# A two-layer diffusion trunk on one core: expert value rows fetched in blocks of 32 slots of four tokens, and the row slots dealt anew to the stages

## The reference, cut to what matters

```
h = layer_norm(x) * (1 + scale_a) + shift_a
t = token_mix(h)                  # attention | retention | RWKV-7 scan, gates, branches, output
x = layer_norm(ALPHA*x + gate_a*t)
h = layer_norm(x) * (1 + scale_f) + shift_f
x = layer_norm(ALPHA*x + gate_f*peer(h))
```

```
ts, ti = top_k(scores, 16)                       # of 128 keys, two halves per head
fs, fpos = top_k(ts[0] + ts[1], 16)              # of the candidate sums
eidx = picked index; g = softmax(fs)             # (n, 128)
act = gelu(einsum('nkd,nd->nk', u[eidx], x)) * g # a product per slot
out = einsum('nk,nkd->nd', act, v[eidx])         # weighted sum of v rows
```

## Time and profile before

| | |
|---|---|
| median of 3 runs | 4228.18 us (4217.14 to 4244.32) |
| the profiled execution, time of its run | 4215.97 us |
| its span | 4214.2 us |
| moved by its transfers | 1077.41 MB, 256 GB/s over the span |
| TensorE, VectorE, GpSimd busy | 63%, 50%, 42% |
| u fetches, v fetches | 768 each |

### The profile page before, as it was taken

How to read it: one execution, slowest core, us unless ns; L and a number is a source line. 1 busy time by engine, 2 the same in 40 slices (tenths; PEclk the granted TensorE clock), 3 DMA queues, 4 the chain that set the end, 5 groups by cost and what they waited for, 6 DMA issues and landing times.

```text
span 4214.2 us, 52812 instructions
## 1 busy us (share of the span) xinstructions
PE 2670.3 (63%) x21467; PEld 1660.6 (39%) x21467; DVE 2117.1 (50%) x5314; ACT 550.1 (13%) x1415; POOL 1749.7 (42%) x1738
## 2 busy tenths in 40 slices
PE   5878478488977344556788737847897400455576
PEld 1767456366743234112354225636674200000011
DVE  4352588743033899455511168874403699433201
ACT  0231111321000010021010011132100100000000
POOL 1000355322322356666644445542232356666564
PEclk9989689599988666677899868968998755677799
DMA  8506678544866779987989867853486578999897
GB/s 320 200 5 237 165 282 313 191 141 152 295 217 225 264 267 344 347 306 274 322 314 360 293 175 282 308 203 127 152 296 224 182 227 289 347 331 322 299 349 279
DMA packets 346467, 1077.41 MB, mean 256 GB/s; under 512 B 30466, under 2 KB 34696, under 8 KB 346096
## 3 DMA queue, kind: packets, MB, share of 16 engines
q0 software_dynamic: 231168, 829.37, 56.5%
q1 hardware_dynamic: 115056, 244.66, 16.1%
HBM read 1070.24 MB, written 3.67 MB: 255 GB/s over the span
## 4 chain that ended last, share of the span: by engine, by line
PE 37%; DVE 23%; DMA 22%; POOL 10%; issue 5%; ACT 2%; SPq 0%; DVEq 0%; ACTq 0%
DMA arena<-in_peer_v,arena 14%; PE ps L2123 10%; POOL arena L1998 9%; DVE arena L2050 7%; PE ps L1551 5%; PE ps L568 5%; DMA arena<-in_peer_u,arena 3%; DMA ring<-in_w_mod 3%; PE ps L1564 2%; DVE arena L1844 2%; PE ps L1577 2%; PE ps L1279 1%; PE ps L1660 1%; DVE arena L1838 1%; PE ps L1287 1%
## 5 line engine op out<-in xcount | busy, mean ns | idle before, releaser
L1998 POOL DMA_INDIRECT arena<-in_peer_u,arena x768 | 875.9, 1141 | 753.6 <-DVE arena L2050 464.8
L1998 POOL DMA_INDIRECT arena<-in_peer_v,arena x768 | 752.6, 980 | 1041.8 <-PE ps L2123 811.9
L2050 DVE CUSTOM_DVE_ANT_1 arena<-arena,hT 128x1024 f32<-128x1024 f32 x768 | 922.4, 1222 | 437.5 <-DMA arena<-in_peer_u,arena 427.6
L2123 PE MATMUL ps<-arena 128*32 128x512 f32 x3072 | 825.3, 692 | 495.3 <-DMA arena<-in_peer_v,arena 406.1
L568 PE MATMUL ps<-hT,ring 128*128 128x256 f32 (+1 forms) x2496 | 499.8, 366 | 268.7 <-DVE arena L592 259.0
L2123 PEld LDWEIGHTS ps<-arena 128*32 128x32 f32 x3072 | 140.8, 117 | 1091.6 <-issue 508.0
L568 PEld LDWEIGHTS ps<-hT,ring 128*128 128x128 f32 x2496 | 434.3, 221 | 328.2 <-DVE arena L592 265.3
L1551 PE MATMUL ps<-hT,ring 128*128 128x128 f32 (+1 forms) x1536 | 261.2, 329 | 2.6 <-DMA ring<-in_w_in 1.3
L1551 PEld LDWEIGHTS ps<-hT,ring 128*128 128x128 f32 x1536 | 231.8, 191 | 47.8 <-issue 26.9
L1598 DVE TENSOR_TENSOR arena<-ps,arena 128x128 f32<-128x128 f32 (+1 forms) x32 | 11.5, 358 | 389.5 <-PE ps L1564 389.5
L2024 DVE TENSOR_TENSOR arena<-ps,gate 128x512 f32<-128x512 f32 x12 | 8.3, 692 | 389.8 <-PE ps L2123 389.6
(11 more groups left out here) (342 smaller groups left out, 3602.1 us busy)
## 6 DMA issues: line engine op xcount, KB each, us to landing
ring<-in_w_in SPq DMA_DIRECT2D x60, 2048.0 KB, 11.2
ring<-in_w_mod SPq DMA_DIRECT2D x24, 2048.0 KB, 9.2
ring<-in_w_br SPq DMA_DIRECT2D x12, 2048.0 KB, 12.0
ring<-in_w_out SPq DMA_DIRECT2D x8, 2048.0 KB, 12.4
ring<-in_peer_wq SPq DMA_DIRECT2D x8, 2048.0 KB, 9.6
arena<-in_peer_u,arena POOLq DMA_INDIRECT x768, 6.4
arena<-in_peer_v,arena POOLq DMA_INDIRECT x768, 6.2
ring<-in_w_in SPq DMA_DIRECT2D x4, 1536.0 KB, 15.2
```

Of the source, the lines that this page charges most:

```text
L1998: pool.indirect_dma_start(rowbuf[i % NB], None, v_rows if which else u_rows, bass.IndirectOffsetOnAxis(ap=offset, axis=0))\
L2050: nc.vector.tensor_tensor_reduce(row, row, tile_cols(hT, t), 1.0, 0.0, ALU.mult, ALU.add, row_dot[t][:, k:k + 1]).then_inc(sem("u_used"), 1)
L2123: ins = nc.tensor.matmul(row_acc[c][32 * g:32 * g + 32, :], strip[j % 2][:, g, 31 - j:63 - j], rows[g][:, 512 * c:512 * (c + 1)], start=(j ...
```

## The change

A v fetch now takes, instead of 128 slots of one token, 32 slots of each of four tokens: partition 32b+i gets slot 32q+i of token 32b+j, which is what VectorE's 32 x 32 block transpose of the picks gives. So block q of a tile needs only the picks and weights of slots 32q to 32q+31. Quad n of a tile is in block n//8, and the first stands in slot 43 instead of 143. The transposes on TensorE go; VectorE transposes blocks of picks (24 of them, L1948 of the new file) and of weights (24, L2078), and writes the strip (192 times, 16 numbers per partition, L2087) that ScalarE wrote. Since the rows of the accumulators now stand in another order, ScalarE copies them out (2 copies per tile) and 8 more products per tile with rows of the unit matrix put them in order. END is 175 for p's experts and 315 for s's. The table of stages:

| stage | in s mixes, slots before | now | in p1, before | now |
|---|---|---|---|---|
| mod | none | none | none | 0 to 24 |
| projection | 0 to 110 | 0 to 42 | 0 to 150 | 24 to 122 |
| retention | 110 to 130 | 42 to 46 | 150 to 180 | 122 to 132 |
| preparation | 130 to 142 | 46 to 48 | 180 to 200 | 132 to 138 |
| scan | 142 to 192 | 48 to 100 | 200 to 260 | 138 to 198 |
| merge | 192 to 280 | 100 to 180 | 260 to 420 | 198 to 318 |

```diff
+    parts["block"] = p[:, None] // 32 == np.arange(4)[None]
...
-RIDE = {"s": {"proj": (0, 110, 39), "ret": (110, 130, 2), "prep": (130, 142, 3), "scan": (142, 192, 24), "merge": (192, 280, 60)},
-        "p": {"proj": (0, 150, 39), "ret": (150, 180, 2), "prep": (180, 200, 3), "scan": (200, 260, 12),
-              "merge": (260, 420, 60)}}
+RIDE = {"s": {"mod": (0, 0, 10), "proj": (0, 42, 39), "ret": (42, 46, 2), "prep": (46, 48, 3), "scan": (48, 100, 24),
+              "merge": (100, 180, 60)},
+        "p": {"mod": (0, 24, 10), "proj": (24, 122, 39), "ret": (122, 132, 2), "prep": (132, 138, 3), "scan": (138, 198, 12),
+              "merge": (198, 318, 60)}}
...
@@ pe_mod and dve_mod, likewise on GpSimd and ScalarE @@
             for c in chunks:
+                pump("dve", "mod", c)
                 dve.wait_ge(sem("mod_mm"), 12 * l + c + 1)
...
-                nc.vector.tensor_scalar(row_f[t][:, TOPK * h0:TOPK * (h0 + nh)], ij[:, 0, :], float(l * NKEYS * NKEYS),
-                                        None, ALU.add)
                 nc.vector.tensor_scalar(row_no[t][:, TOPK * h0:TOPK * (h0 + nh)], ij[:, 0, :], float(l * NKEYS * NKEYS),
                                         None, ALU.add).then_inc(sem("chosen"), 1)
+                dve.wait_ge(sem("chosen"), at("chosen", u + 1))
+                for q in range(h0 // 2, (h0 + nh) // 2):
+                    cols = slice(32 * q, 32 * q + 32)
+                    nc.vector.transpose(row_noT[t][:, cols], row_no[t][:, cols]).then_inc(sem("no_T"), 1)
...
-            def turn_at(t):
-
-                return 134 + 140 * t
-
-            def quad_at(t, j):
-
-                return turn_at(t) + 6 + 4 * j + 3
+            def start_at(t, q):
+
+                return P * t + 32 * q + 40 + 12 * t
+
+            def quad_at(t, n):
+
+                q, i = divmod(n, 8)
+                return start_at(t, q) + 4 * i + 3
...
-                return 32 * (m % 4) + m // 4
-
-            END = quad_at(nt - 1, 31) + 3
+                q, n = divmod(m, 32)
+                return 32 * q + 8 * (n % 4) + n // 4
+
+            END = quad_at(nt - 1, 31) + 8
...
@@ dve_rows @@
-                        if v == turn_at(t) + 2:
-                            dve.wait_ge(sem("rows_T"), at("rows_T", t + 1))
-                            nc.vector.tensor_copy(row_noT[t], row_acc[0][:, 0:P]).then_inc(sem("no_T"), 1)
-                        if v == quad_at(t, 31) + 1:
+                        for q in range(4):
+                            if v == start_at(t, q) - 3:
+
+                                cols = slice(32 * q, 32 * q + 32)
+                                dve.wait_ge(sem("row_w"), at("row_w", 8 * t + 2 * q + 2))
+                                link(nc.vector.transpose(row_wT[t][:, cols], row_dot[t][:, cols]))
+                        for n in range(32):
+                            if v == quad_at(t, n) - 3:
+                                if 32 * t + n >= 2:
+                                    dve.wait_ge(sem("v_used"), at("v_used", 32 * t + n - 1))
...
+                                nc.vector.tensor_tensor(strip[n % 2][:, :, 28:32], w.to_broadcast([P, 4, 4]),
+                                                        K("block").rearrange("p (o g) -> p o g", o=1).to_broadcast([P, 4, 4]),
+                                                        ALU.mult).then_inc(sem("strip"), 1)
+                        if v == quad_at(t, 31) + 5:
                             residual(t)
...
@@ act_rows @@
+                        if v == quad_at(t, 31) + 1:
+                            act.wait_ge(sem("v_used"), at("v_used", 32 * (t + 1)))
...
+                            for c in range(2):
+                                nc.scalar.activation(sums[c], row_acc[c][:, :], ACT.Copy).then_inc(sem("sum_out"), 1)
...
@@ pe_rows @@
-                                                               strip[j % 2][:, g, 31 - j:63 - j],
+                                                               strip[n % 2][:, g, 28 - 4 * i:60 - 4 * i],
...
+                        if v == quad_at(t, 31) + 3:
+                            pe.wait_ge(sem("sum_out"), at("sum_out", 2 * t + 2))
+                            for c in range(2):
+                                for g in range(4):
+                                    ins = nc.tensor.matmul(row_acc[c][32 * g:32 * g + 32, :], unmix[:, g, :], sums[c],
+                                                           start=True, stop=True, tile_position=(0, 32 * g))
+                            ins.then_inc(sem("sum_in"), 1)
```

More of the change, by code:

```diff
@@ L347, in pool_params, with act_mod @@
                         .then_inc(sem("param_in"), 16)
+            for c in MOD_PARTS[l, part]:
+                pump("pool", "mod", c)
+        def act_mod(act, l, part, pump):
+            for c in MOD_PARTS[l, part]:
+                pump("act", "mod", c)
         def pe_cond(pe):
@@ L2192, in _ @@
             act_cond(act)
[L2193 removed]
+            program("act", act, act_mod, linker(act, "act"))
         @block.vector
```

65 lines of the change are left out of this document (28 added, 37 removed).

## The result

The median went from 4224.97 us (15 runs, 4214.52 to 4244.32) to 4264.41 us (15 runs, 4248.0 to 4277.13): a ratio of 1.009, with a 95% interval of 1.0077 to 1.0104. The change makes the kernel 0.9% slower, 39 us, where 99 us less were forecast. The 4264 us lie outside the range of 4020 to 4215.

A forecast was written before the change was run, and what follows sets the result against it. No one resource was taken to bound the whole: VectorE, TensorE or transfers by stage, transfers in p1 and the last experts. Terms -24 (s0, s1), -37 (p1), -38 (last experts) gave -99: 4117, as a median 4129 us, range 4020 to 4215.

The forecast's parts named there:

- Part 1, projection, retention, preparation: Mixes s0 and s1, each: projection 45 us shorter, retention 20 shorter, preparation 3 longer.
- Part 1, scan: Scan of s0 and s1: u products mostly hidden, fetches with six buffers charged, +25 us each, bounds 0 and 68 + 58.
- (d): Rival: scan of s0 and s1 stops on its fetches, +126 us there and +30 in the gates; 4341 us, chance 0.09.
- the cycle of a quad with six buffers: Scan of s0 and s1: 12.7 us with eight buffers plus two issues of 0.94, so 14.6 us, times 13 = 190.
- Part 1, merge: Gates and rest of s0 and s1: more fetches beside the gate weights, fewer quads behind the scan, +25 us each, bounds 0 and 45.
- Part 2: Mix p1: slots moved into the mod stage, later stages at assumed transfer rates, 1115 us to 1078, -37 us.
- (b): Rival: p1's stages keep their old transfer rates, so p1 gains nothing, +13 us; total 4179 us, chance 0.15.
- Part 3: Last experts: 725 us instead of 767 from slot 43 to the last quad, +4 at the end; -38 us.
- The tail: End of the last experts: two copies and eight products between the last quad and the residual, +4 us.
- Behind it transfers bound, 328 GB/s: Last experts, behind the first quad: transfers taken as the bound, 328 GB/s while u and v fetches alternate.
- Small things: Whole program: strips and block transposes on VectorE, about 41 us, hidden where it waits; bounds 0 and 41 us longer.
- (e): Rival: selection on VectorE delays issuing of fetches, 51 us each in the last experts and p1; 4231 us, chance 0.06.

The follow-up runs named there:

- the short products: Changed kernel with the u products of p's experts cut to 16 of 1024 columns, fetches and waits kept: 4206.1 us in one run, scan of s0 228 us.

## Why the prediction was wrong, step by step

The traces differ by +58 us where the working had -99, so 157 us are to be explained: 85 of them are the scans of s0 and s1, 35 p1 and 37 the last experts.

**Part 1, projection, retention, preparation.** Right: -48 against -45, and -13 against -17. The wait that was to shrink did (TensorE, 457 to 696 us, beside the earlier trace rows):

```profile
PE ps L579 <- DVE arena L603: 27.5, 2, 27.1
```

**Part 1, scan.** This is the step that failed first and most: "+25" was +70 in s0 and +65 in s1. The rival of the slower side, (d), named the mechanism, and it came at a part of its price: scan and gates together cost 105 and 98 us, where (d) had 156. It was given a chance of 0.09. The term that was too small is the cycle of a quad with six buffers, 14.6 us; 17.0 were measured. The working took the cycle of eight buffers and added two issues at 0.94, but from one issue to the next GpSimd takes 1.24. The loop itself, added up anew, is five such steps, landing and the last products, 5 x 1.24 + 5.7 + 1.9 = 13.8 us. The same sum gives 15.8 for five buffers (a landing and a u product come in: 5.7 + 1.2 + 1.24 + 5.7 + 1.9; measured 19.7), 11.8 for half rows in six (14.0) and 9.3 in eight (12.5): 2 to 4 us low each time, with steps between them that go the right way. The rest is not taken apart by any run; the waits of GpSimd for u products, of up to 15.7 us, suggest that VectorE and TensorE come to a landed row only between steps of the levels. 13 x 17.0 is 221 of the 233 us of the window: the scan goes at the pace of the fetches. Had VectorE's work been the cause, the short products would have given back more than 13.

**Part 1, merge.** Right in sum: gates +35, the rest -12, against +25.

**Part 2.** The mod stage +49 against +40, projection -1 against +6, retention and preparation -111 against -108: right. Scan and merge fell short: 192 and 362 us where 173 and 347 were forecast, so -2 instead of -37. The working let them run at 328 and 334 GB/s; they had 293 and 317. For the merge rival (b), that p1 keeps its rates, is what came (361 us); the scan was longer than even (b)'s 177. With buffers freed by row p1 takes 1046 us with the same bytes and order of fetches, so it was not the transfers that could give no more.

**Part 3.** Here nearly all of the forecast failed to come: -38, and the last experts gave 1. From slot 43 to the last quad's end it took 758.6 us, where 725 were forecast and 767 had been. Of the 34 us 11 are the alternating quads (49 at 13.02 and 12.78 instead of 12.7), 8 the turn from one tile to the other (32 us instead of 24), 7 the 13 quads alone, which came every 6.6 us instead of 6.04, and 7 the first quad, which the sum left out: it has 62 of the 64 quads. The tail took 31 us instead of 23, where +4 was forecast. The start of GpSimd's first store, of the changed kernel:

```profile
4259.02 0.58 POOL L2208 DMA_DIRECT2D out<-X  x1 [24.89 <-DVE X L2099]
```

and of the kernel before:

```profile
4205.69 0.58 POOL L2181 DMA_DIRECT2D out<-X  x1 [21.49 <-DVE X L2070]
```

The step from the last quad to it grew from 14.3 to 17.4 us, about as forecast. From the first store to the end it is 13.7 us instead of 8.5, but the stores landed after the same 5.1 and 3.0 us in both kernels. What grew is the closing drain of GpSimd's queue behind them, 7.6 us instead of 2.4. It is 7.6 us in every run with the new fetches and 2.4 in both without; what makes it so is open.

Behind the size stands a reading. "Behind it transfers bound, 328 GB/s" took a rate for a limit because the transfers were busy at 0.92. With buffers freed by row the same transfers moved 386. What the fetches had was eight buffers, each used once a cycle; the cycle was set by the loop above, and the rate came out of it: 8 x 0.524 MB in 12.7 us is 330 GB/s. A run of u fetches at 1.79 us (179/100) had little to gain from such a cycle at 1.6 a fetch, and that was in the rows. The rates of p1 in Part 2 rest on the same reading.

The Trainium skill's limit of about 358 GB/s from memory per core (DMA: Bandwidth & Descriptors, Specifications), weighed in the prediction, does not hold here: 386 GB/s stood for 300 us in the run with rows freed. Another page of the Trainium skill (Perfetto Trace Analysis, Engine Utilization, Roofline) says that a single active core on trn2 can pull more than that share, up to its 16 transfer engines' sum of about 435 GB/s; the 386 agree with that.

**Small things and (e).** Reordering and strips cost nothing that shows. With selection beside the fetches the mean issue in the alternating stretch was 1.03 us (256.7/249) instead of 0.99 (219.9/223), some 0.4 us a cycle, where (e) would have had 3.6.

**What stays open.** With rows freed and the change's own table, the scan is at 231 us. The waits put it down to u products, and five or eight buffers show that the number counts, but whole rows in eight buffers did not fit and weren't run. Nor is the cause of the longer drain at the end known. That quads alone come every 5.4 us in the mean in the changed order, and every 5.1 in the old one, is a single step of 8.7 us, in which GpSimd loads two rows of parameters between the fetches; the others are 5.0 to 5.7 us long.

## What to carry to other kernels

Before a stretch is called bound by transfers, write down the loop of one buffer: issue, landing, use, release, and which of them the next issue waits for. If bytes under way divided by the time of that loop gives the measured rate, the rate is a result, and releasing earlier or holding more buffers is worth more than moving the fetches about. A release that waits for the last of several rows costs the issues and the landing of all of them, and where fewer buffers stand it costs more, so this layout, which brings the fetches forward, paid only once the release was cut.

## What the runs showed of the hardware

Gathers of 128 rows of 4 KB issued by GpSimd went on at 386 GB/s on one core, the transfers busy at 1.00, with a mean of 1.35 us from issue to issue (300/222). Half rows of 2 KB landed 3.7 us after their issue, whole ones after 5.7 in the scan and 6.0 to 6.4 in the last experts (medians), so by these two sizes in the scan some 1.7 us of a landing don't depend on the bytes (3.7 - 2.0, an estimate from few landings). One issue after another without a wait took GpSimd 1.24 us a fetch with whole rows and 1.25 with half ones.
